# More row buffers for the dense expert stage of layer 0, and its late loads one at a time

## The reference, cut to what matters

```python
def peer_ffn(h, wq, subkeys, u_tab, v_tab):      # one block of 128 tokens:
    q = (hb @ wq).reshape(PEER_BLOCK, PEER_HEADS, 2, PEER_DK // 2)
    ...                                          # two top-16 lists a head, top 16 of their sums: idx, g
    a = gelu(einsum('td,thkd->thk', hb, u_tab[idx]))        # 8 heads x 16 experts a token
    return einsum('thk,thkd->td', (g * a), v_tab[idx])
```

## Time and profile before

| | us |
|---|---|
| median of 3 runs | 5278.07 |
| lowest, highest | 5274.64, 5282.68 |
| span of the profiled execution | 5287.0 |
| TensorE busy in it | 4755.0 (90%) |
| VectorE busy | 3167.6 (60%) |
| GpSimd busy | 1960.1 (37%) |

### The profile page before, as it was taken

The page is one execution under the profiler, slowest core; times in us unless marked ns, Lnnn a source line. Parts: engine busy times, 40 slices in busy tenths (PEclk is TensorE's granted clock), DMA queues, the critical chain, the costliest instruction groups (busy, mean ns, idle before and its releaser), DMA issues.

```text
span 5287.0 us, 76501 instructions
## 1 busy us (share of the span) xinstructions
PE 4755.0 (90%) x25470; PEld 3886.5 (74%) x25470; DVE 3167.6 (60%) x6165; ACT 1580.6 (30%) x3001; POOL 1960.1 (37%) x1948
## 2 busy tenths in 40 slices
PE   8888889999988886999998987799999987999998
PEld 4557578898988885665655655568898986888886
DVE  1563363757558876266665725616475756677777
ACT  1221241353433338000000012314244348222332
POOL 1110121000048876377777511103100007576652
PEclk9888999999999999999999997799999999999999
DMA  3221112565648992699999932111355561899997
GB/s 150 85 98 48 44 33 101 165 210 164 201 161 319 341 365 78 220 377 369 376 371 382 405 135 80 64 56 41 119 170 189 182 195 42 305 368 349 350 374 266
DMA packets 316677, 1103.39 MB, mean 209 GB/s; under 512 B 59392, under 2 KB 108672, under 8 KB 267872
## 3 DMA queue, kind: packets, MB, share of 16 engines
q1 hardware_dynamic: 165024, 648.09, 34.5%
q0 software_dynamic: 151488, 453.35, 23.3%
HBM read 1037.13 MB, written 62.03 MB: 208 GB/s over the span
## 4 chain that ended last, share of the span: by engine, by line
PE 60%; DVE 10%; POOL 10%; issue 8%; DMA 8%; ACT 2%; POOLq 1%; DVEq 0%; ACTq 0%; PEldq 0%; SPq 0%
PE PS L1184 14%; PE PS L1249 12%; DMA arena<-in_experts,arena 7%; PE PS L1273 6%; POOL arena L638 6%; PE PS L1143 5%; PE PS L872 4%; PE PS L875 4%; PE PS L1258 4%; POOL arena L644 3%; PE PS L1105 3%; DVE PS L2290 3%; PE PS L937 1%; PE PS L994 1%; PE PS L916 1%
## 5 line engine op out<-in xcount | busy, mean ns | idle before, releaser
L1184 PE MATMUL PS<-hS,wS 128*128 128x256 f32 x9216 | 1169.4, 291 | 110.6 <-DVE wS L2315 77.2
L1184 PEld LDWEIGHTS PS<-hS,wS 128*128 128x128 f32 x9216 | 1154.0, 199 | 125.4 <-DVE wS L2315 87.8
L2290 DVE SCALAR_TENSOR_TENSOR PS<-arena,PS 128x1024 f32<-128x1024 f32 x762 | 979.7, 1286 | 332.3 <-DMA arena<-in_experts,arena 309.6
L638 POOL DMA_INDIRECT arena<-hx,arena x768 | 843.4, 1098 | 397.4 <-issue 229.4
L644 POOL DMA_INDIRECT arena<-in_experts,arena x768 | 773.5, 1007 | 519.1 <-DVE PS L2290 306.5
L1249 PE MATMUL PS<-hS,ring 128*128 128x256 f32 x4096 | 927.0, 380 | 3.1 <-POOLq L382 3.1
L1249 PEld LDWEIGHTS PS<-hS,ring 128*128 128x128 f32 x4096 | 780.4, 191 | 164.9 <-issue 60.3
L2315 DVE TENSOR_TENSOR wS<-ring,wS 128x1024 fp32r<-128x1024 f32 x384 | 469.8, 1224 | 327.6 <-ACT wS L1542 326.8
L1258 PE MATMUL PS<-ring,arena 128*128 128x512 f32 x1024 | 469.2, 602 | 52.2 <-DVE arena L2434 52.2
L1648 ACT ACTIVATE arena<-PS 128x256 f32<-128x256 f32 x256 | 98.2, 384 | 1192.6 <-PE PS L1249 1192.6
L1542 ACT ACTIVATE wS<-ring 128x1024 fp32r<-128x1024 f32 x384 | 403.5, 1052 | 8.7 <-DMA ring<-in_experts 5.1
(11 more groups left out here) (302 smaller groups left out, 5403.6 us busy)
## 6 DMA issues: line engine op xcount, KB each, us to landing
ring<-in_experts SPq DMA_DIRECT2D x256, 1024.0 KB
ring<-in_experts SPq DMA_DIRECT2D x384, 512.0 KB
ring<-in_wcat SPq DMA_DIRECT2D x80, 1024.0 KB
hx<-arena SPq DMA_DIRECT2D x384, 128.0 KB, 3.0
ring<-in_wq SPq DMA_DIRECT2D x40, 1024.0 KB
arena<-in_rpb POOLq DMA_DIRECT2D x96, 128.0 KB, 2.6
arena<-hx,arena POOLq DMA_INDIRECT x768, 6.3
arena<-in_experts,arena POOLq DMA_INDIRECT x768, 7.5
```

The costliest lines, as they stand in the source:

```text
L638: pool.indirect_dma_start(out=aX[n][:, k:k + 1], out_offset=None, in_=src, in_offset=bass.IndirectOffsetOnAxis(ap=at[:, k:k + 1], axis=0)) ...
L1184: mm = pe.matmul(bank[6 + c % 2][:, 0:PASS], u[:, k, :], hS[:, h, k, :], start=(part == 0 and k == 0), stop=(part == 2 and k == KD - 1))
L2290: op = dve.scalar_tensor_tensor(out=total, in0=row, scalar=aX[n][:, k:k + 1], in1=total, op0=ALU.mult, op1=ALU.add)
```

## The change

1. `hS`'s second half, `wS` and `gS_` lie behind one another and together have 7 x 1024 columns. They become seven row buffers in layer 0 (`spare`), free from the start; four more follow in the arena at chunks 4, 8, 12, 16. The nine of layer 1 stay.
2. With these, `row_plan` gives 3 rows a chunk from chunk 0 on (step 3.03125), and the last rows at chunk 126 as before.
3. Three rows (`HELD`) are issued already in `gbuild`, behind its activation gathers and ahead of the drain. They go to the half of `hS` and to `gS_`, which `gbuild` does not use.
4. The late loads, of both layers, are issued one by one: each has a chunk from which its place is free (56 to 92), waits for `gfull` of that chunk, and is issued before the row that is due six chunks later.

The diff, less the lines that only pass the new names on:

```diff
 def buffers_free(layer):
-    return [4 + 4 * j for j in range(9)]
+    return [0] * SPARE + [4 + 4 * j for j in range(4)] if layer < DEPTH - 1 else [4 + 4 * j for j in range(9)]
...
-            have = sum(f + lead <= c for f in free)
+            have = sum(not f or f + lead <= c for f in free)
...
-        ready = [j for j, f in enumerate(free) if f + lead <= c]
+        ready = [j for j, f in enumerate(free) if not f or f + lead <= c]
...
+        at_split = (nc.sbuf_base + 31) // 32 * 32
         hS = sb("hS", [P, 2, KD, PASS], F32R)
         wS = sb("wS", [P, 4, D], F32R)
         gS_ = sb("gS_", [P, 4, PASS], F32R)
+        assert nc.sbuf_base == at_split + 4 * 9 * D
+        spare = nc.alloc_sbuf_tensor_at("spare", [P, SPARE, D], F32, offset=at_split + 4 * 2 * D)
...
-        NV = 9
+        NV = 11
...
-        vX = view(0, NV, D)
+        vX = [[spare[:, j, :] for j in (0, 1, 6, 2, 3, 4, 5)] + [view(j * D, D) for j in range(4)],
+              [view(j * D, D) for j in range(9)]]
+        HELD = 3
...
                 take_activations(0, late[0], range(ahead, built))
+                due, buf, prev = row_plan(len(late), buffers_free(l))
+                held = HELD if early else 0
+                for r in range(held):
+                    take_row(vX[l][buf[r]], buf[r], vA[:, late[0] % 2], r)
                 end(f"gbuild{l}{b0}")
...
+                homes = [(60, gbP, d["gates"][l, 0:1, D:2 * D].broadcast_to([P, D])),
+                         (92, gbX, (d["gates"][l, 1:2, D:2 * D] if f0 < CB else d["fnw"]).broadcast_to([P, D]))]
+                homes += [(84 + 4 * i, xr[:, i, :], d["xs"][(b0 + i) * P:(b0 + i + 1) * P, :]) for i in range(2)]
+                homes += [(68 + 4 * i, xrX[:, i, :], d["xs"][(f0 + i) * P:(f0 + i + 1) * P, :]) for i in range(b0 - f0)]
+                if early:
+                    homes.append((56, yX[3], ys))
+                homes.sort(key=lambda home: home[0])
                 for r, (b, k) in enumerate(order):
...
-                    if r == due[100]:
-                        pool.wait_ge(s["gfull"], dn * PK + 97)
...
+                    while homes and r >= due[homes[0][0] + 6]:
+                        c, dst, src = homes.pop(0)
+                        pool.wait_ge(s["gfull"], dn * PK + c)
+                        pool.dma_start(dst, src).then_inc(s["gate_in"], 16)
+                    if r < held:
+                        continue
+                    if prev[r] >= 0:
+                        pool.wait_ge(s["acc_done"], rows0 + prev[r] + 1)
+                    elif buffers_free(l)[buf[r]]:
                         pool.wait_ge(s["gfull"], dn * PK + buffers_free(l)[buf[r]])
-                    else:
-                        pool.wait_ge(s["acc_done"], rows0 + prev[r] + 1)
-                    take_row(vX[:, buf[r], :], buf[r], v_at[b], k)
-                assert not later
+                    take_row(vX[l][buf[r]], buf[r], v_at[b], k)
+                assert not later and not homes
```

More of the change, by code:

```diff
@@ L33 @@
 LEVELS = 7
+SPARE = 7
 EPS = 1e-6
@@ L722, in _ @@
                 v_at = {b: (vC if early and b >= f0 + 2 else vA)[:, b % 2] for b in late}
-                due, buf, prev = row_plan(len(late), buffers_free(l))
                 rest = [(n, k) for n in range(len(late)) for k in range(built if n == 0 else 0, P)]
@@ L2422, in next_row @@
                             weigh(n, k // 32, t["gates"])
-                        add_row(n, yX[n], vX[:, buf[r], :], buf[r], k)
+                        add_row(n, yX[n], vX[l][buf[r]], buf[r], k)
                     def step(c):
```

## The result

The changed kernel takes 5218.01 us (median of 4 runs, 5216.94 to 5221.62); the kernel before, run beside it, 5278.23 (4 runs, 5274.64 to 5282.68). The ratio is 0.9886, with a 95% interval of 0.9872 to 0.9900. The forecast was 5222.

The account below looks back on a forecast made before the run. GpSimd's issue in the middle and a burst of late loads were taken to hold up layer 0's dense stage. 69.1 us go, 6 + 4 + 3 = 13 come: -56, 5231 us in a profile, 5222 as median; range 5213 to 5232.

Parts of the forecast that it names:

- The step of the middle is GpSimd's issue: Layer 0's dense stage, 2400 to 2860 us: 6.12 issues a chunk at 1.255 us each set the step, 7.69 us.
- rival 2: GpSimd stays the bound: at 1.30 us an issue 7.02 us a chunk, 14.6 us more, 5237 us; chance 0.09.
- (a): Layer 0's dense stage, 2400 to 2860 us: 60 chunks each 0.785 us too long, 47.1 us, all to go.
- (b): Layer 0's dense stage, 2865 to 2902 us: nine late loads in one burst cost TensorE 20.1 us, to go.
- small waits outside (a) and (b): Rest of the 69.1 us lost in layer 0's dense stage: 2 us, expected to go too.
- +6 for the barrier: Before layer 0's dense stage: the drain waits for three held rows to land; cost 6 us, between 3.8 and 23.
- +4 for the slip of the first rows: Start of layer 0's dense stage: rows 5, 8, 11 land late for TensorE; cost 4 us, between 0 and 9.
- +3 for the late loads one by one: Layer 0, chunks 60 to 98: nine spread loads add issue time and 4.7 MB; cost 3 us, between 0 and 9.
- From profile to median: Profiled span was 8.9 us over the median before; same difference kept, so 5231 us in a profile, 5222 as median.
- rival 1: DMA engines become the bound at 372 GB/s with gathers beside: -39, 5239 us; chance 0.12.
- rival 3: No gain: the engines sustain only 358 GB/s over layer 0's dense stage, 947 us, 5275 us in all; chance 0.05.
- rival 4: Slower: seven rows in flight lower the DMA rate below 357 GB/s; at 350, 5296 us; chance 0.05.

Follow-up runs that it names:

- experiment 5: The kernel before with every second activation gather between rows of layer 0's dense stage left out; 5443.19 us on chip A, ratio 0.9766.
- experiment 8: The kernel before with SP fetching 512 KB more for every second chunk of layer 0; 5601.61 us on chip A, ratio 1.0040.
- experiment 4: The changed kernel with ScalarE's chunk loop written out and GpSimd leaving the stage ahead of each dense one without a drain; 5217.91 us on chip D, ratio 0.9884.
- experiment 1: The changed kernel as it is, run again on chip D beside the kernel before; 5219.27 us, ratio 0.9885.
- experiment 3: The changed kernel with ScalarE's loop over the chunks of the dense stages written out; 5221.39 us on chip D, ratio 0.9884.
- experiment 6: The changed kernel with the late loads in one burst again; 5536.55 us on chip A, ratio 0.994; loop written out too on C, 0.9924.
- experiment 7: The kernel before with only the late loads issued one by one; 5584.65 us on chip A beside 5579.42, ratio 0.9989.

## Why the prediction was right

The time came within 4 us of the forecast, and the mechanism is the one forecast: both losses of the stage went, and little but the barrier came in their place. That it came so close is in part luck: several small terms were off, and they cancelled. By its steps:

- **The step of the middle is GpSimd's issue.** 7.67 us a chunk became 6.89, with the engines at 395 GB/s against 372 and a row landing 8.2 us after issue at the median against 7.5. So 372 was not what the engines could give with gathers beside; it was what GpSimd asked of them. Nor were the nine buffers short: GpSimd's waits for VectorE there were the ordinary 0.3 us, 12.2 us in 40 waits. The price of an issue stayed 1.25 us, and the new plan's need of 6.77 us a chunk just fits. How closely shows in a sign that did not come: in this stretch GpSimd's idle time did not shift from "issue" to waiting for VectorE. It still goes back to back, as rival 2 had it, but without making the step longer, and a kernel with more issues a chunk would wait for it again. Experiments 5 and 8, on chips where ScalarE waits, could not test this step.
- **-47 for (a) and -20 for (b).** TensorE's idle time inside the stage fell to nothing, and both terms are seen whole. Whether (b) would have gone by the earlier rows alone was not measured on a chip without ScalarE's waits.
- **-2 for "small waits outside (a) and (b)".** This did not come. The stage is 883.9 us, 2.4 over the 881.5 of its products, and all of it is in the first 32, which take 9.31 us where 32 take 6.9 at full clock. Before they took 8.59: the small loss was for the most part the clock of 0.5 to 0.6 behind the barrier and no wait, and the longer idle time made it 0.7 larger (experiment 4, after 0.72 us of idle time: clock 1.00, 7.17 us). No run takes the idle time alone away.
- **+6 for the barrier.** It measured 11.7 us for 6.2, so +5.5. Its parts: the third row is issued 3.76 us behind the last activation gather, lands 5.2 us later, and the drain ends 2.8 us after that, where the step took 3.7. That the drain holds the barrier after the last issue is borne out by experiment 4: without it the idle time ahead of the stage drops from 8.33 to 0.72 us.
- **+4 for the slip of the first rows.** It was 0, and this is the term that was mis-sized. Its issue times held: rows 5, 8 and 11 were issued 11.7, 19.3 and 25.8 us after the stage began, where it had 11.5, 19.0 and 25.6. Its landing was too short: row 5, the first tight one, was issued at 2135.19 and taken by VectorE at 2143.97, 8.8 us later, where 5.8 was taken and 7.5 weighed. By the step's own deadline (2123.45 + 16.84 = 2140.29) that is 3.7 us late, just the 4 of the forecast. But the deadline, the decisive part, was 4 us too early: between the GELU of the chunk (2139.68) and that chunk's eight products (2146.37) TensorE has not 2.2 us of other work, but the eight products of the chunk before and the sixteen of the next, 6.7 us. So VectorE waited 4.62 us for row 5, and its gated product was still done 0.8 us before TensorE came for it. In experiment 4, where the stage starts sooner against the loads that the first gathers need (first gather 5.2 us after it, for 4.1) and the first products are quicker, those 0.8 us are gone and a slip of 2.8 appears.

GpSimd's issues of rows 3, 4 and 5 (timeline of the changed kernel):

```profile
2131.44 0.94 POOL L650 DMA_INDIRECT spare<-in_experts,arena  x1 [0.30 <-issue]
2133.94 0.94 POOL L650 DMA_INDIRECT spare<-in_experts,arena  x1 [0.30 <-issue]
2135.19 0.95 POOL L650 DMA_INDIRECT spare<-in_experts,arena  x1 [0.30 <-issue]
```

What VectorE, ScalarE and TensorE make of row 5 (timelines of the three engines):

```profile
2143.97 1.29 DVE L2299 SCALAR_TENSOR_TENSOR PS<-spare,arena,PS 128x1024 f32<-128x1024 f32 x1 [4.62 <-DMA spare<-in_experts,arena]
2145.16 0.42 DVE L2443 TENSOR_TENSOR arena<-arena 128x256 f32<-128x256 f32 x1
```

```profile
2139.68 0.38 ACT L1657 ACTIVATE arena<-PS 128x256 f32<-128x256 f32 x1 [6.50 <-PE PS L1258]
```

```profile
2139.48 3.60 PE L1267 MATMUL PS<-ring,arena 128*128 128x512 f32 x8
2142.92 3.62 PE L1258 MATMUL PS<-hS,ring 128*128 128x256 f32 x16
2146.37 3.60 PE L1267 MATMUL PS<-ring,arena 128*128 128x512 f32 x8
```

- **+3 for the late loads one by one.** It was 0. They add 5.4 us of issue and land after 7.1 to 9.5 us; the engines carried up to 406 GB/s in single stretches of 22 us while activation gathers ran too, over the 389 that the bound had been set by. A lead, on which the step had counted, there was hardly: VectorE waited for a row 84 times in the middle. What covered the loads was the time that VectorE has in hand before TensorE wants its product, as for row 5. Here are the bytes moved in the 40 slices of the stage:

```profile
GB/s 134 375 395 377 386 393 396 383 376 387 393 385 382 394 393 387 378 394 386 398 390 405 384 397 403 401 401 403 403 404 406 401 378 396 416 414 411 415 340 0
```

- **Layer 1: 0.** With its loads spread TensorE is busy 785 of 785 us from 4400 to 5185, so they cost nothing.
- **From profile to median.** The sum gave -56 in the span; it was -67.1. From the last activation gather before the barrier to the end of the stage it is 895.7 us for 956.9, which is -61.2: the -56, the two zeros above (-7) and half a microsecond at the barrier, less the 2.4 that stayed at the start. Another 1.8 went in the stages before, which the change doesn't touch (the last activation gather starts at 2111.68, not 2113.51), and 4.1 behind the stage, of which 1.8 is a wait of TensorE's in layer 1 that the profile after doesn't show; the rest was not traced. In medians it was only -60.2: the span of the profiled execution of before is 8.9 over its median, and that of after 1.9 over. I had carried the 8.9 over as if it were the profiler's. More likely it was the spread of the kernel before, whose 13 runs on chip D lie 19 us apart; the four runs of experiments 1, 3 and 4 lie 4, 8 and 10 apart. The two misses nearly cancelled in the time.
- **The rivals.** Rivals 1, 3 and 4 needed the engines to stop at 372, 358 or below 357 GB/s with gathers beside; 460 us at 395 refute all three. With rival 3 falls, for this program on one core, the rule of the Trainium skill that was weighed there ("DMA: Bandwidth & Descriptors", section "Where 436 GB/s comes from": some 358 GB/s per core from HBM). Rival 2 needed GELUs 7.0 us apart, and they are 6.89.

The kernel without the drain (experiment 4) has the shortest span, 5213.0 us, yet its median, 5217.91, differs from those of the changed kernel (5218.01, and 5219.27 on D) by less than the spread of the runs.

**What stays open.** What ScalarE waits for on chips A, B and C: the trace says "remote", it is not the loop's jump, and in the three traces of A it ends with the activation gathers. And what the spreading of the late loads is worth at full pace, since the kernels that would tell (experiments 6 and 7) ran on such chips only. For the same reason no experiment at full pace takes issues or bytes alone; there the two traces, before and after, carry the argument.

## What to carry to other kernels

A DMA share near 1.0 does not say that the DMA engines bind: here the engine that issues them bound, seen by its busy and idle time adding up to the whole stretch with no wait longer than the 0.3 us between two issues, and by landings of 7.5 us at the median, not far over the 5.8 of a lighter load and well under the 16.4 where it did wait for buffers. If an issuing engine has idle time early in a stage and is short of it later, buffers that let it start earlier can return the shortage, as the 47 us here. The price is at the barrier, where the drain waits for what has been issued last. And when you ask how late an input may come, count all the work that the engine behind it still has in order, not only the nearest piece.

## What the runs showed of the hardware

- GpSimd's drain after three gathered rows of 512 KB held the barrier until 7 us after GpSimd was done issuing the last of them (2116.38 to 2123.40), 2.8 us after it had landed. In experiment 4 a plain instruction with the same signal let TensorE start 0.13 us after the last issue.
- One core moved 395 GB/s for 460 us with small gathers beside, and 411 to 416 over four slices of 22 us with rows and expert tiles alone.
- The same kernel takes 5 to 6% longer on some chips: 5536 to 5590 us in place of 5278 to 5285. The traces of its variants show there waits of ScalarE for "remote" before the GELU of the dense stages, 222 to 562 us in all, and none on the chip without the loss.
- TensorE's first 32 products after the barrier took 9.31 us after 7.67 us of idle time, 8.59 after 2.18, and 7.17 after 0.72. The granted clock was 0.50 for some 4 us in the first case, 0.50 for under 3 us in the second, and 1.00 throughout in the third.
